# 48 of 256 prompt tokens leave the down product of the PEER layers and join the decoded tokens, by way of DRAM scratch and gathered v rows

## The chip, the core and the metric

The kernel runs on one core of a Trainium2 chip. The metric is the device time of one launch in microseconds (us). The core's engines run side by side: TensorE (PE: matmuls, and PEld, its loads of stationary operands), VectorE (DVE), ScalarE (ACT), GpSimd (POOL) and SyncE (SP, which issues most DMAs). They meet only at semaphores.

## The reference, cut to what matters

Two decoder layers run over 256 prompt tokens and 8 decoded ones (T = 264, D = 1024). Each layer ends in a PEER expert mixer, and its two large products are what the change is about:

```python
def one_block(xb):
    q = einsum('td,de->te', xb, w_q).reshape(128, 8, 2, 128)
    s = einsum('thpc,hpkc->thpk', q, subkeys)
    v1, i1 = top_k(s[:, :, 0], 16); v2, i2 = top_k(s[:, :, 1], 16)
    ...
    eidx = ...                      # 8 heads x 16 = 128 experts of 16384 for each token
    gates = softmax(top_s, axis=-1).reshape(128, 128)
    h = gelu(einsum('td,ted->te', xb, u_tab[eidx]))
    w = gates * h
    return einsum('te,ted->td', w, v_tab[eidx])
```

The result goes through `x <- LayerNorm(alpha*x + f(x))`. `u_tab` and `v_tab` hold 16384 rows of 1024 fp32 numbers for each layer.

## The kernel before, in words

For prompt tokens the kernel does not gather experts. It computes the activation of all 16384 experts for all tokens and multiplies by a gate matrix that is zero but for the chosen ones. The experts are taken as 128 slabs ("rows" below) of 128 experts: a slab is 128x1024 fp32, 512 KB, and a ring of 4 slots holds four. All products are made of three matmuls on split operands (high x high, high x low, low x high; type fp32r), which keeps fp32 accuracy.

`peer_up` makes, slab by slab, `big[:, n, :]` (experts x tokens): ACT writes the high part of the u slab (L2024), POOL the low part (L1930), PE runs 24 matmuls with 264 moving columns (L1972 to L1974) into one of two banks, ACT applies gelu on the way to `big` (L2028, or L2040 and L2041 once gates are there). From slab 52 to 122 the gates of the 256 prompt tokens are formed in 64 groups of four tokens: one-hot matrices on DVE and ACT, a gate product on PE (L1993: 4 fp32 matmuls, which the trace records as 8), ACT and DVE apply it. SP loads the u slabs in order, each as its slot comes free, and at the end of the block the first four v slabs (`load_until`, L203).

`peer_down` multiplies the gated activations of the 256 prompt tokens by the v slabs. Stationary are 128 tokens of `wh`/`wl` (the two parts of `big[:, n, 0:256]`), moving are 512 columns of the v slab's parts `hi`/`lo`: 2 halves x 2 token tiles x 3 = 12 matmuls for a slab (L2386 to L2388). ACT makes `hi` (L2326) and `wh` (L2325), DVE `lo` (L2354) and `wl` (L2350). `hi` has four half-slab buffers, so ACT and DVE run up to two slabs ahead of PE.

The 8 decoded tokens are dealt with apart. Their 128 chosen experts each are spread over 128 partitions as 8 units. ACT copies their activations out of `big` (L2328), SP stores them to a DRAM scratch `decoded_hidden` (L2287), POOL gathers by indirect DMA the v rows (L2304: one unit is 128 rows of 4 KB, 4 buffers) and the activations (L2310: 128 numbers for a unit). DVE, in its program after slab 10, waits for all gathered activations, multiplies them by their gates and builds `own`, 32 stationary columns for each unit. PE adds one unit after each of slabs 12 to 19 (`values`, L2396; unit j writes partitions 32(j%4) and on of banks 6 and 7), and after slab 23 sums the four parts (`add_groups`, L2403). `peer_norm` then copies the prompt result out of banks 0 to 3, transposes it back on PE (L2444), adds the residual (L2449) and normalises.

Each block ends in a barrier of all five engines. Every engine runs its own instructions strictly in the order written; only the semaphores name who waits.

Of the kernel before, what the change touches and what calls it, by code (L numbers as in the profile page):

```python
# [23 lines left out]
F32 = mybir.dt.float32  # L24
F32R = mybir.dt.float32r
# [62 lines left out]
class Step:  # L88


    def __init__(self, nc, io, top):
# [35 lines left out]
        self.hidden = nc.dram_tensor("decoded_hidden", (P, NKEYS * TS), F32, kind="Internal").ap()  # L127
# [1691 lines left out]


def peer(step, layer):
    nc, io, ps = step.nc, step.io, step.ps
    L = f"_{layer}"
    with ExitStack() as ctx:
        big = step.sb("expert_activations" + L, [P, NKEYS, T], ctx=ctx)
        rows = step.sb("decoded_expert_rows" + L, [P, 2, TOPK // 2], U32, ctx=ctx)
        gates = step.sb("decoded_gates" + L, [P, TOPK // 2], ctx=ctx)

        flat = big[:].rearrange("p n t -> p (n t)")
        end = NKEYS * T  # L1830
# [10 lines left out]
GROUPS = TP // GROUP  # L1841
# [14 lines left out]
def peer_up(step, layer, big, qT, scratch, keys_ready, row_index, row_gate):  # L1856
# [9 lines left out]
    gelu_part = step.squares[:, 3:5, 0:TP]  # L1866
# [10 lines left out]
    with ExitStack() as c1, nc.Block("peer_up" + L, no_gpsimd_drain=True) as block:  # L1877
# [4 lines left out]
        row_f = step.sb("decoded_rows_float" + L, [P, 2, TOPK], ctx=c1)  # L1882
        token_of = step.sb("decoded_token" + L, [P, TS], ctx=c1)[:]
# [22 lines left out]
        s_wm = step.sem("activations_gated" + L)  # L1906
        half_done = lambda n, g: 2 * (ub + n) + g + 1

        @block.sync
        def _(sp):  # L1910
            with sp.Fori(1, NKEYS // SLOTS) as i:
                for s in range(SLOTS):

                    sp.wait_ge(step.u_product, half_done(SLOTS * i + s - SLOTS, 1))
                    sp.dma_start(step.ring[:, s, :], io["u"][layer * P + SLOTS * i + s]).then_inc(step.slab_ready[s], 16)
            step.loaded = base + NKEYS
            step.load_until(sp, base + NKEYS + SLOTS)
# [99 lines left out]
        def _(act):  # L2017
# [8 lines left out]
            def gelu(i, s):  # L2026
                act.wait_ge(step.u_product, half_done(SLOTS * i + s, 1))
                nc.scalar.activation(big[:, SLOTS * i + s, :], ps[:, s % 2, 0:T], ACT.Gelu_apprx_tanh).then_inc(s_g, 1)  # L2028

            def gelu_in_parts(n):  # L2030

                gated = GROUP * groups_before(n)
                if gated == 0:
                    gelu(n // SLOTS, n % SLOTS)
# [6 lines left out]
                nc.scalar.activation(big[:, n, gated:T], bank[:, gated:T], ACT.Gelu_apprx_tanh).then_inc(s_g, 1)  # L2041
# [24 lines left out]
            with act.Fori(0, PLAIN // SLOTS) as i:  # L2066
                for s in range(SLOTS):
                    ahead = (i, s + 2) if s < 2 else (i + 1, s - 2)
                    high(*ahead, 0)
                    gelu(i, s)  # L2070
                    high(*ahead, 1)
            act.wait_ge(s_rt, 3)
# [18 lines left out]
        def _(dve):  # L2091
# [79 lines left out]
            for t, (w, heads) in enumerate(((pick[:, 0, 2, :], PH), (pick[:, 1, 2, :], PH), (pick_s[:, 2, :], 1))):  # L2171
# [10 lines left out]
            link(nc.vector.scalar_tensor_tensor(out=row_f[:, 0, :], in0=pick_s[:, 1, :], scalar=float(NKEYS), in1=pick_s[:, 0, :],  # L2182
                                                op0=ALU.mult, op1=ALU.add))
# [387 lines left out]
```

## Time and profile before

| | |
|---|---|
| median of 3 runs | 2500.17 us (2498.72 to 2501.71) |
| profiled execution, its own time | 2500.44 us |
| span of that execution in the trace | 2498.7 us |
| busy of the span | PE 95%, PEld 85%, DVE 67%, ACT 52%, POOL 40% |
| granted TensorE clock, mean | 0.968 of 2.4 GHz |
| bytes moved by DMA | 409.30 MB, 164 GB/s over the span |
| `peer_up` of the two layers, first to last matmul | 441 to 890 us, 1638 to 2088 us |
| `peer_down` of the two layers, first to last matmul | 894.5 to 1275 us, 2092 to 2473 us |

The 1.7 us between the span and the profiled execution's own time lie outside the instructions. Matmuls are pipelined: a record's duration (284 ns for 264 columns) is longer than the distance between two starts, and the distance is what a matmul costs in a row of them.

### The profile page before, as it was taken

What the parts mean: (1) busy time and instruction counts of PE and PEld (TensorE: products, weight loads), DVE (VectorE), ACT (ScalarE), POOL (GpSimd) and SP (SyncE); (2) the same over time, 40 slices, a digit from 0 to 9 for tenths busy, and PEclk for the clock granted to TensorE, in tenths of its full rate; (3) what the DMA queues carried; (4) which work ended last, traced back from release to release, by engine and by line L of the source; (5) the groups of instructions that cost most, each with busy time, mean ns of one, the idle gap of its engine ahead of it and who ended that gap; (6) DMA issues with size and microseconds to landing.
All of it is one profiled execution on the core that took longest, in us unless ns stands there. A gap on an engine that the chain in (4) does not pass through costs nothing. (4 is left out here: it accounts for less than half of the span.)

```text
span 2498.7 us, 46290 instructions
## 1 busy us (share of the span) xinstructions
PE 2361.9 (95%) x15692; PEld 2114.0 (85%) x15692; DVE 1675.8 (67%) x3447; ACT 1290.7 (52%) x2924; POOL 1010.0 (40%) x777
## 2 busy tenths in 40 slices
PE   8798989999999999999979988999999999999997
PEld 8686869999999976888858886999999998688885
DVE  4544748996988844666653454899698894466665
ACT  5221536445776654555543343644577765455554
POOL 4441433898777730000011033479877775000000
PEclk9995999999999999999989989999999999999999
DMA  6333745444444464555535375544444446455552
GB/s 227 131 110 43 261 183 176 148 160 160 141 141 142 142 214 167 186 187 188 185 102 169 100 261 201 180 146 160 162 142 137 143 144 205 167 187 187 187 185 93
DMA packets 115075, 409.30 MB, mean 164 GB/s; under 512 B 19977, under 2 KB 22193, under 8 KB 109489
## 3 DMA queue, kind: packets, MB, share of 16 engines
q1 hardware_dynamic: 110896, 391.45, 47.0%
q0 software_dynamic: 4032, 15.86, 1.9%
q8 instruction: 96, 1.57, 0.3%
q14 instruction: 51, 0.42, 0.1%
HBM read 397.11 MB, written 10.14 MB: 163 GB/s over the span
## 5 line engine op out<-in xcount | busy, mean ns | idle before, releaser
L1930 POOL TENSOR_TENSOR slab_ring_lo<-slab_ring,u_hi 128x512 fp32r<-128x512 f32 x512 | 708.3, 1402 | 203.7 <-ACT u_hi L2024 203.1
L1972 PE MATMUL banks<-operand_hi,u_hi 128*128 128x264 f32 x2048 | 594.6, 290 | 18.5 <-POOL slab_ring_lo L1930 18.4
L1974 PE MATMUL banks<-operand_hi,slab_ring_lo 128*128 128x264 f32 x2048 | 583.1, 285 | 0.0
L1973 PE MATMUL banks<-operand_lo,u_hi 128*128 128x264 f32 x2048 | 581.9, 284 | 0.0
L2354 DVE TENSOR_TENSOR operand_lo<-slab_ring,operand_hi 128x512 fp32r<-128x512 f32 x512 | 354.3, 692 | 134.2 <-ACT operand_hi L2326 129.0
L2386 PE MATMUL banks<-operand_hi,w_hi 128*128 128x512 f32 x1024 | 410.2, 401 | 8.0 <-DVE w_lo L2350 8.0
L309 POOL TENSOR_TENSOR slab_ring_lo<-slab_ring,slab_hi 128x512 fp32r<-128x512 f32 x112 | 146.4, 1308 | 668.8 <-ACT slab_hi L299 668.7
L2388 PE MATMUL banks<-operand_lo,w_hi 128*128 128x512 f32 x1024 | 407.9, 398 | 0.0
L2387 PE MATMUL banks<-operand_hi,w_lo 128*128 128x512 f32 x1024 | 407.8, 398 | 0.0
L1972 PEld LDWEIGHTS banks<-operand_hi,u_hi 128*128 128x128 f32 x2048 | 386.6, 189 | 23.1 <-POOL slab_ring_lo L1930 18.7
L2024 ACT ACTIVATE u_hi<-slab_ring 128x512 fp32r<-128x512 f32 x512 | 321.7, 630 | 159.1 <-PE banks L1974 156.5
L2326 ACT ACTIVATE operand_hi<-slab_ring 128x512 fp32r<-128x512 f32 x512 | 319.3, 624 | 140.6 <-PE banks L2388 140.6
L1973 PEld LDWEIGHTS banks<-operand_lo,u_hi 128*128 128x128 f32 x2048 | 385.5, 188 | 0.0
L1974 PEld LDWEIGHTS banks<-operand_hi,slab_ring_lo 128*128 128x128 f32 x2048 | 385.1, 188 | 0.0
L2386 PEld LDWEIGHTS banks<-operand_hi,w_hi 128*128 128x128 f32 x1024 | 194.1, 190 | 68.4 <-DVE w_lo L2350 21.8
L2388 PEld LDWEIGHTS banks<-operand_lo,w_hi 128*128 128x128 f32 x1024 | 194.1, 190 | 47.5
L2387 PEld LDWEIGHTS banks<-operand_hi,w_lo 128*128 128x128 f32 x1024 | 194.3, 190 | 46.6
L2350 DVE TENSOR_TENSOR w_lo<-expert_activations,w_hi 128x256 fp32r<-128x256 f32 x256 | 108.9, 425 | 164.0 <-ACT w_hi L2325 163.8
L2325 ACT ACTIVATE w_hi<-expert_activations 128x256 fp32r (+1 forms) x256 | 106.8, 417 | 211.5 <-PE banks L2388 211.5
L331 PE MATMUL banks<-operand_hi,slab_hi 128*128 128x264 f32 x496 | 148.3, 299 | 40.9 <-DVE operand_lo L579 15.9
L299 ACT ACTIVATE slab_hi<-slab_ring 128x512 fp32r<-128x512 f32 x220 | 131.4, 623 | 92.5 <-PE banks L333 57.4
L2211 DVE TENSOR_SCALAR one_hot_rows<-constants,squares 128x128 f32<-128x128 f32 x344 | 177.9, 577 | 0.0
(351 smaller groups left out, 4010.7 us busy)
## 6 DMA issues: line engine op xcount, KB each, us to landing
slab_ring<-in_u SPq DMA_DIRECT2D x256, 512.0 KB, 3.3
slab_ring<-in_v SPq DMA_DIRECT2D x256, 512.0 KB, 3.2
slab_ring<-in_proj SPq DMA_DIRECT2D x144, 512.0 KB, 3.3
cache_k_T<-in_cache_k SPq DMA_DIRECT2D x16, 1024.0 KB, 8.8
cache_v<-in_cache_v SPq DMA_DIRECT2D x16, 1024.0 KB, 13.1
memory_T<-in_mem POOLq DMA_DIRECT2D x2, 1024.0 KB, 6.7
sample_state<-in_state POOLq DMA_DIRECT2D x1, 2048.0 KB, 9.1
out_mem_k_out<-mem_k_T SPq DMA_DIRECT2D x16, 128.0 KB, 2.2
```

The lines of the kernel that those rows point to most:

```text
L331: nc.tensor.matmul(out, wh[:, c, :], xh[:, c, :], start=(c == 0), stop=False)
L1930: nc.gpsimd.tensor_tensor(step.ring_lo[:, s, g * HC:(g + 1) * HC, :], step.slab(s)[:, g * HC:(g + 1) * HC, :], hi[:, buf].bitcast(F32), AL ...
L1972: nc.tensor.matmul(bank, hi[:, buf, k, :], xh[:, c, :], start=(c == 0), stop=False)
L1973: nc.tensor.matmul(bank, hi[:, buf, k, :], xl[:, c, :], start=False, stop=False)
L1974: last = nc.tensor.matmul(bank, step.ring_lo[:, s, c, :], xh[:, c, :], start=False, stop=(c == DC - 1))
L2024: nc.scalar.activation(hi[:, buf], step.slab(s)[:, g * HC:(g + 1) * HC, :], ACT.Copy).then_inc(s_hi, 1)
L2211: last = nc.vector.tensor_scalar(rows[g % NB][:, k, :], step.iota, selT[:, 0, token], selT[:, 2, token], ALU.is_equal, ALU.mult)
L2326: nc.scalar.activation(hi[:, (2 * s + g) % 4, :], step.ring[:, s, g * HALF:(g + 1) * HALF], ACT.Copy).then_inc(s_hi, 1)
L2354: nc.vector.tensor_tensor(lo[:, buf, :], step.ring[:, s, g * HALF:(g + 1) * HALF], hi[:, buf, :].bitcast(F32), ALU.subtract).then_inc(step ...
L2386: nc.tensor.matmul(bank, wh[:, b, ts], hi[:, buf, :], start=first, stop=False)
L2387: nc.tensor.matmul(bank, wl[:, b, ts], hi[:, buf, :], start=False, stop=False)
L2388: last = nc.tensor.matmul(bank, wh[:, b, ts], lo[:, buf, :], start=False, stop=final)
```

## The change

`GATHERED = 48` prompt tokens (208 to 255) are treated like the decoded ones in the down product, so that 56 tokens (`GT`) take the gathered way and 208 (`TD`) the dense one.

- `peer_up` still multiplies all 264 columns. Gelu is written in two instructions: columns up to 208 to `big`, the last 56 to a small buffer `part`, which SP stores to the DRAM scratch four slabs at a time (32 stores of 128 x 896 bytes in a layer). SP waits for all stores before it issues the first v slabs.
- Gates are formed for 208 tokens only: 52 groups in place of 64, over the same slabs.
- `peer_down` swaps the operands: stationary are 128 columns of the v slab, moving are 208 tokens, 8 x 3 = 24 matmuls for a slab. The result comes out in the layout of the residual, so the copies and transposes of `peer_norm` are gone.
- There are 56 units in place of 8, gathered into 8 buffers, and added in batches of four, one matmul to each quarter of the partitions: 14 batches, after slabs 26, 33, ..., 117. DVE waits for the 56 gathered activations after its part of slab 23.
- The program of PE for `peer_down` is written out for all 128 slabs, where it had a loop from slab 28.

```diff
-GROUPS = TP // GROUP
+GROUPS = TD // GROUP
...
         @block.sync        # peer_up
...
+            def store(c, half):
+                sp.wait_ge(s_g, SLOTS * c + SLOTS)
+                sp.dma_start(chunk_of[c], part[:, half]).then_inc(s_out, 16)
...
+            for c in range(NKEYS // SLOTS - 2, NKEYS // SLOTS):
+                store(c, c % 2)
+            sp.wait_ge(s_out, 16 * (NKEYS // SLOTS))
             step.loaded = base + NKEYS
             step.load_until(sp, base + NKEYS + SLOTS)
...
+            def gelu_later(n, i, s, half, reused):
+
+                if s == 0 and reused:
+                    act.wait_ge(s_out, 16 * (i - 1))
+                nc.scalar.activation(part[:, half, s, :], ps[:, s % 2, TD:T], ACT.Gelu_apprx_tanh).then_inc(s_g, 1)
...
-OWN_AT, VALUES_FROM, SUM_FROM, UNROLLED = 10, 12, 22, 28
+UNITS = TS + GATHERED
+BATCH = 4
+OWN_AT, BATCH_FROM, BATCH_EVERY = 24, 26, 7
+COPY_AT, ADD_AT, LAST_AT = 120, 122, 124
...
         @block.gpsimd      # peer_down
...
+            for u in range(NB):
+                fetch(u)
+            for u in range(UNITS):
+                nc.gpsimd.indirect_dma_start(hidden[:, u:u + 1], None, hidden_of,
+                                             bass.IndirectOffsetOnAxis(row_index[:, 1, u:u + 1], 0)).then_inc(s_hid, 16)
+            for u in range(NB, UNITS):
+                pool.wait_ge(s_val, (u - NB) // BATCH + 1)
+                fetch(u)
...
         @block.vector      # peer_down
...
+            for n in range(OWN_AT):
+                low(n // SLOTS, n % SLOTS)
...
+            dve.wait_ge(s_hid, 16 * UNITS)
...
+            with dve.Fori(OWN_AT // SLOTS, NKEYS // SLOTS) as i:
                 for s in range(SLOTS):
                     low(i, s)
...
-                    for t in range(2):
-                        bank, ts = ps[:, 2 * t + g, :], slice(t * P, (t + 1) * P)
-                        nc.tensor.matmul(bank, wh[:, b, ts], hi[:, buf, :], start=first, stop=False)
-                        nc.tensor.matmul(bank, wl[:, b, ts], hi[:, buf, :], start=False, stop=False)
-                        last = nc.tensor.matmul(bank, wh[:, b, ts], lo[:, buf, :], start=False, stop=final)
+                    for k in range(HC):
+                        cs = slice(k * P, (k + 1) * P)
+                        out = dense(g * HC + k)
+                        nc.tensor.matmul(out, hi[:, buf, cs], wh[:, b, :], start=(n == 0 and k % 2 == 0), stop=False)
+                        nc.tensor.matmul(out, hi[:, buf, cs], wl[:, b, :], start=False, stop=False)
+                        last = nc.tensor.matmul(out, lo[:, buf, cs], wh[:, b, :], start=False, stop=(n == NKEYS - 1 and k % 2 == 1))
```

How the order of instructions moves is seen at three places. First SP at the end of `peer_up`, where the loads of the first v slabs stand; `in_u` and `in_v` are the expert tables. Before:

```order
L1915 DMA slab_ring<-in_u 128x1024
L1911 REGISTER_ALU
L1911 COMPARE_AND_BRANCH
L203 DMA slab_ring<-in_v 128x1024 x4
L1877 UNCONDITIONAL_BRANCH
L2284 UNCONDITIONAL_BRANCH
L2287 DMA decoded_hidden<-squares 128x1024
```

And SP at the same place with the change:

```order
L1922 DMA slab_ring<-in_u 128x1024 x4
L1926 DMA gathered_hidden<-gathered_hidden_part 128x224 x2
L203 DMA slab_ring<-in_v 128x1024 x4
L1881 UNCONDITIONAL_BRANCH
L2332 UNCONDITIONAL_BRANCH
```

The last stores of activations moved from behind the v loads to ahead of them, and the last of them needs the gelu of slab 127.

Second POOL in `peer_down`: the indirect DMAs that fetch v rows (`in_v`) and activations (into `squares`), first before and then with the change (a row stands for as many instructions as its last number says).

```order
L2296 UNCONDITIONAL_BRANCH
L2298 MEMSET squares 128x256
L2304 DMA gathered_rows<-in_v,decoded_expert_rows 128x1024 x4
L2310 DMA squares<-decoded_hidden,decoded_expert_rows 128x1 x8
L2304 DMA gathered_rows<-in_v,decoded_expert_rows 128x1024 x4
```

```order
L2342 UNCONDITIONAL_BRANCH
L2344 MEMSET own_columns 128x1792
L2349 DMA gathered_rows<-in_v,gathered_expert_rows 128x1024 x8
L2354 DMA squares<-gathered_hidden,gathered_expert_rows 128x1 x56
L2349 DMA gathered_rows<-in_v,gathered_expert_rows 128x1024 x48
```

Ahead of the last activation now stand 8 fetches and 55 gathers where there were 4 and 7, and the memset is seven times as wide.

Third DVE at the end of its part of slab 23, with the change; L2412 is the instruction that waits for all gathered activations (before, its like stood after slab 10).

```order
L2395 TENSOR_TENSOR w_lo<-expert_activations,w_hi 128x208
L2399 TENSOR_TENSOR operand_lo<-slab_ring,operand_hi 128x512
L2412 TENSOR_TENSOR squares<-squares,gathered_gates 128x56
L2415 TENSOR_TENSOR own_columns<-squares 128x8x8
L2417 COPY own_columns<-squares 128x12x4
L2418 UNCONDITIONAL_BRANCH
L2418 ISA
L2399 TENSOR_TENSOR operand_lo<-slab_ring,operand_hi 128x512
```

Behind it in DVE's order stand the low parts of slab 24 and all later ones.

## Rows read from the trace of the kernel before

**Rows 1.** Busy time by stretch: us, busy by engine, clock, DMA share, GB/s

```profile
core 0: us, PE busy (x) PEld busy (x) DVE busy (x) ACT busy (x) POOL busy (x), PEclk, DMA share, GB/s
700.00:800.00 100.00, 100.00 (x840) 100.00 (x839) 86.46 (x161) 69.74 (x193) 72.44 (x54) 1.00 0.44 143
...
892.00:930.00 38.00, 35.49 (x141) 28.45 (x142) 23.84 (x43) 21.21 (x41) 12.35 (x13) 0.91 0.73 246
```

**Rows 2.** Timeline of the down product: start, us, engine, line, operation

```profile
1099.92 0.39 PE L2386 MATMUL banks<-operand_hi,w_hi 128*128 128x512 f32 x1
...
1110.47 0.39 PE L2386 MATMUL banks<-operand_hi,w_hi 128*128 128x512 f32 x1
```

**Rows 3.** Timeline of the up product, a slab with a gate product

```profile
801.35 0.28 PE L1973 MATMUL banks<-operand_lo,u_hi 128*128 128x264 f32 x1
...
804.05 0.28 PE L1974 MATMUL banks<-operand_hi,slab_ring_lo 128*128 128x264 f32 x1
804.05 0.98 PEld L1993 LDWEIGHTS banks<-one_hot_columns,one_hot_rows 128*128 128x128 f32 x8
...
804.95 0.19 PEld L1972 LDWEIGHTS banks<-operand_hi,u_hi 128*128 128x128 f32 x1
...
805.06 0.19 PEld L1973 LDWEIGHTS banks<-operand_lo,u_hi 128*128 128x128 f32 x1
...
805.18 0.28 PE L1973 MATMUL banks<-operand_lo,u_hi 128*128 128x264 f32 x1
```

**Rows 4.** Weight loads of 32 columns in attention: ns min/median/max

```profile
L1684 PEld LDWEIGHTS banks<-cache_k_T,sample_own_rows x256: 106/110/110, 317.3 to 1528.4; 128*32 128x32 f32 x128
```

**Rows 5.** Timeline of PE in attention, matmuls to four partition quarters in turn

```profile
317.35 1.93 PE L1684 MATMUL banks<-cache_k_T,sample_own_rows 128*32 128x256 f32 x32
```

**Rows 6.** Timeline of PE around a unit of the decoded tokens

```profile
933.38 0.40 PE L2388 MATMUL banks<-operand_lo,w_hi 128*128 128x512 f32 x1
933.71 1.90 PE L2396 MATMUL banks<-gathered_rows,squares 128*32 128x512 f32 x4
935.54 0.50 PE L2386 MATMUL banks<-operand_hi,w_hi 128*128 128x512 f32 x1
```

**Rows 7.** Timeline from the last gelu to the first down matmul

```profile
890.83 0.17 ACT L2041 ACTIVATE expert_activations<-banks 128x8 f32<-128x8 f32 x1
...
892.78 0.61 ACT L2326 ACTIVATE operand_hi<-slab_ring 128x512 fp32r<-128x512 f32 x1
...
894.51 0.80 PE L2386 MATMUL banks<-operand_hi,w_hi 128*128 128x512 f32 x1 [4.00 <-DVE w_lo L2350]
```

**Rows 8.** DMA issues: engine, count, KB each, median us to landing

```profile
slab_ring<-in_v SPq DMA_DIRECT2D x256, 512.0 KB, 3.2
...
out_mem_k_out<-mem_k_T SPq DMA_DIRECT2D x16, 128.0 KB, 2.2
...
squares<-decoded_hidden,decoded_expert_rows POOLq DMA_INDIRECT x16, 4.2
```

**Rows 9.** Timeline of POOL in the down block, both layers

```profile
891.81 0.31 POOL L2298 MEMSET squares<- 128x256 f32 x1 [4.75 <-POOLq L1877]
892.59 1.05 POOL L2304 DMA_INDIRECT gathered_rows<-in_v,decoded_expert_rows  x1 [0.47 <-POOL squares L2298]
...
898.01 0.95 POOL L2310 DMA_INDIRECT squares<-decoded_hidden,decoded_expert_rows  x1 [0.30 <-issue]
...
906.91 1.26 POOL L2310 DMA_INDIRECT squares<-decoded_hidden,decoded_expert_rows  x1 [0.30 <-issue]
...
2096.16 0.99 POOL L2310 DMA_INDIRECT squares<-decoded_hidden,decoded_expert_rows  x1 [1.02 <-DMA decoded_hidden<-squares]
...
2106.21 0.94 POOL L2310 DMA_INDIRECT squares<-decoded_hidden,decoded_expert_rows  x1 [0.30 <-issue]
```

**Rows 10.** Timeline of the tail, layer 1, up to the mean's subtraction

```profile
2473.27 1.29 DVE L2431 COPY expert_activations<-banks 128x512 f32<-128x512 f32 x2 [4.28 <-PEq L2260]
...
2474.47 0.21 DVE L2432 SCALAR_TENSOR_TENSOR res_peer<-x_T,squares 128x64 f32<-128x64 f32 x1
...
2481.38 2.80 DVE L395 TENSOR_TENSOR res_peer<-res_peer,banks 128x264 f32<-128x264 f32 x8 [0.81 <-PE banks L380]
```

More of the change, by code:

```diff
@@ L1865, in peer_up @@
     selT = step.squares[:, 0:3, 0:TP]
-    gelu_part = step.squares[:, 3:5, 0:TP]
+    gelu_part = step.squares[:, 3:5, 0:TD]
     at = 2 * PH * P
@@ L1910, in _, with load @@
         def _(sp):
[L1911 to L1915, printed above, removed]
+            chunk_of = step.hidden.rearrange("p (c s) t -> c p s t", s=SLOTS)
+            def load(i, s):
+                sp.wait_ge(step.u_product, half_done(SLOTS * i + s - SLOTS, 1))
+                sp.dma_start(step.ring[:, s, :], io["u"][layer * P + SLOTS * i + s]).then_inc(step.slab_ready[s], 16)
+            def store(c, half):
+                sp.wait_ge(s_g, SLOTS * c + SLOTS)
+                sp.dma_start(chunk_of[c], part[:, half]).then_inc(s_out, 16)
+            with sp.Fori(0, NKEYS // SLOTS // 2 - 1) as ii:
+                for half in range(2):
+                    for s in range(SLOTS):
+                        load(2 * ii + 1 + half, s)
+                    store(2 * ii + half, half)
+            for s in range(SLOTS):
+                load(NKEYS // SLOTS - 1, s)
+            for c in range(NKEYS // SLOTS - 2, NKEYS // SLOTS):
+                store(c, c % 2)
+            sp.wait_ge(s_out, 16 * (NKEYS // SLOTS))
             step.loaded = base + NKEYS
@@ L2065, in _, with plain @@
                     high(0, s, g, first=True)
-            with act.Fori(0, PLAIN // SLOTS) as i:
+            def plain(i, half, reused):
                 for s in range(SLOTS):
@@ L2069, in _ @@
                     high(*ahead, 0)
-                    gelu(i, s)
+                    gelu(i, s, half, reused)
                     high(*ahead, 1)
+            for i in range(2):
+                plain(i, i, False)
+            with act.Fori(1, PLAIN // SLOTS // 2) as ii:
+                for half in range(2):
+                    plain(2 * ii + half, half, True)
             act.wait_ge(s_rt, 3)
@@ L2452, in peer_down, with gathered_residual @@
-        emit_norm(step, block, "peer" + L, layer * 3 + 2, res, (0, 1), residual_steps, transposes,
-                  step.used if layer + 1 < LAYERS else None, {"scalar": scalar_early, "vector": vector_early})
+        def gathered_residual(dve):
+            nc.vector.scalar_tensor_tensor(out=res[:, :, TD:T], in0=step.x[:, :, TD:T], scalar=ALPHA, in1=y_g,
+                                           op0=ALU.mult, op1=ALU.add)
+        def residual_steps(dve, j):
+            return nc.vector.scalar_tensor_tensor(out=res[:, j, 0:TD], in0=step.x[:, j, 0:TD], scalar=ALPHA,
+                                                  in1=dense(j), op0=ALU.mult, op1=ALU.add)
```

222 lines of the change are left out of this document (101 added, 121 removed).

## The prediction

> **What bounds the kernel now.** I read the busy times by stretch first. PE is busy for all of 100 us in the middle of the up product and for 35.49 of 38 us at the start of the down product, at a granted clock of 1.00 (2.4 GHz) and 0.91 [rows 1]. So TensorE sets the pace, and the question is what a slab costs on it. That comes from the timeline, by distances between starts. In the down product 45 matmuls of 512 columns pass between 1099.92 and 1110.47, 0.2344 us each [rows 2], 12 of them 2.813 us a slab. In the up product 22 distances of 264 columns take 2.70 us, 0.1227 us each, and a slab with a gate product takes 805.18 - 801.35 = 3.83 us against 24 x 0.1227 = 2.945 without, so a group costs PE 0.885 us [rows 3]. Both widths stream 2.15 to 2.18 columns a ns. The other engines matter where PE waits for them: at the seam between the two products [rows 7] and at whatever the gathered way makes late.
>
> **The change part by part, for one layer.** The sum is made against the profiled execution's 2500.44 us (span 2498.7 and 1.7 outside), which is 0.3 above the median, so I count the two as equal.
>
> 1. *The dense product.* 24 x 208 = 4992 columns take the place of 12 x 512 = 6144. By columns alone a matmul would cost 208 / 2.185 = 0.095 us. But there are now 24 loads of 128 stationary columns, not 12. The eight loads of a gate group start at 804.05 and the next load at 804.95, 0.1125 us apart, though their matmuls have only 128 columns; two fp32r loads behind them start 0.11 apart (804.95, 805.06) [rows 3]. A load seems to go on at that rate beside matmuls, and at 264 columns it is just hidden (0.1227). At 208 columns it no longer is. I take 0.111 us, between the two: 2.664 us a slab, 0.149 less than now. With the two slabs that run at the half clock left out (parts 5 and 6), 126 x 0.149 = **-18.8 us**. Bounds: 0.095 below (columns alone), 0.1227 above (208 columns should not cost more than 264).
>
> The load itself can be priced in another way: a load of 128 columns shows 0.19 us [rows 3], one of 32 columns 0.110 [rows 4], so 96 columns cost 0.080 and 128 cost 0.107 us, if nothing is lost between loads. A slab would be 2.56 us, 13.1 us less in a layer than by 0.111. The Trainium skill, "TensorE: Matmul & The Clock Gate", section "LDWEIGHTS (loading the stationary operand)", puts a load at its column count over 1.2 GHz, whatever the contraction; for 128 columns that is 0.1067 us, and an estimate of the slab by it would be 2.56 us. The row of back-to-back loads says 0.1125, so I stay at 0.111 and make the lower figure a rival.
>
> 2. *Units on PE.* One unit costs 935.54 - 933.38 - 0.234 = 1.93 us now [rows 6], 8 make 15.4. A batch issues 8 matmuls, two for each partition quarter. In attention, 32 records of 256 columns that go to the four quarters in turn take 1.93 us together [rows 5]; one after the other at the same rate they would take several times that, so four run at once. A batch should then cost what a unit costs, 1.95 us. 14 batches are 27.3: **+11.9 us**. Were they serial, a batch would be four units, 7.7 us: +92.
>
> 3. *Gates.* 12 groups fewer on a PE that is full there [rows 1]: 12 x 0.885 = **-10.6 us**.
>
> 4. *Up product otherwise.* ACT gets a second gelu instruction, at least 0.17 us (8 columns) [rows 7]. ACT is busy for 69.74 of 100 us there and PE does not wait [rows 1], so the cover is PE's own 2.9 us a slab; uncovered it would be 128 x 0.17 = 22 us. What is delayed by 0.17 us is the second high part of a u slab and so POOL. I take **+0.5**.
>
> 5. *The seam.* Now the v slabs are in flight when the last gelu ends at 891.00, the first high part starts at 892.78 and PE at 894.51, 1.73 later [rows 7]. After the change SP cannot issue them until the last store has landed. A store of 128 KB lands in 2.2 us, a slab in 3.2 [rows 8]: 891.0 + 2.2 + 3.2 + 1.73 = 898.1, plus 0.1 for issue: **+3.7 us**. The clock loss of the first slabs (0.91 over 38 us, 3.4 us at most, some of it idle [rows 1]) stays; I call it 2.5.
>
> 6. *The gathered activations.* This is the step that a look at bytes misses. POOL restarts 0.8 us after the last engine is done (891.81 against 891.00 [rows 7, 9]), now behind SP: about 894.0. Memset of seven times the columns: 7 x 0.31 = 2.2, and 0.47 to the first DMA: 896.7. Eight fetches at (898.01 - 892.59) / 4 = 1.355 us: 907.5. Activations come at (906.91 - 898.01) / 7 = 1.271 us apart in layer 0 and (2106.21 - 2096.16) / 7 = 1.436 in layer 1, mean 1.354 [rows 9]. 56 of them: 75.8 us, to 983.3, the last landing 4.2 after its start [rows 8]: 986.2. DVE then makes `own` (0.6 us) and the first low part of slab 24 (1.1): PE can start slab 24 at 987.9. It would have arrived at 898.2 + 2.5 + 24 x 2.664 = 964.6. So PE stands still for 23.3 us, and restarts at the half clock, 2.5 more: **+25.8 us**. Behind DVE's wait stand all later low parts, behind them PE, v_split, and with it SP's next v slabs. Bounds: at 1.271 us the stall is 18.7 + 2.5, at 1.436 27.9 + 2.5. Nothing hides it: ACT and DVE are at most two slabs ahead.
>
> 7. *DMA.* In the batch phase 7 slabs and 4 units, 11 x 0.524 MB, pass in 7 x 2.664 + 1.95 = 20.6 us: 280 GB/s. At the start of the down product 246 GB/s kept the DMA engines 0.73 busy [rows 1], which gives about 337 at full share. I take 0, and keep the possibility.
>
> 8. *Tail.* Now 2481.38 - 2473.27 = 8.11 us from the first copy to the mean's subtraction [rows 10]. Without copies and transposes DVE has one instruction of 448 columns (0.21 for 64 [rows 10], so about 0.6) and 8 additions, with the mean's matmuls behind them: about 4.6. **-3.5 us**.
>
> Sum: -18.8 + 11.9 - 10.6 + 0.5 + 3.7 + 25.8 - 3.5 = +9.0 us a layer, +18.0 for two: **2518 us**, 0.7% slower.
>
> **The rivals.**
> - *A load costs 0.107 us.* For it: the differences of durations [rows 3, 4]. Against: the eight loads at 0.1125. 13.1 us less on slabs, but PE arrives 2.5 us earlier at the same wait: -10.6 a layer, 2497 us. By the page's 0.1067 it is the same time to a microsecond. Chance 0.12.
> - *Columns set the pace (0.095 us).* For it: 512 and 264 columns cost the same per column. Against: loads have never been seen closer than 0.11. Slab 2.28 us: 48.4 less, 9.2 given back in the wait, -39 a layer: 2440 us, less whatever DMA (5.77 MB in 17.9 us, 322 GB/s) takes back. This is the side other than mine: faster. It decides from 0.107 us a matmul downward. Chance 0.10.
> - *The wait for activations is not there,* because POOL keeps a much closer pace in a long row of equal gathers. At the measured pace no slack is near; it needs 0.94 us, POOL's busy part alone, or less. Then 56 take 53 us, and the stall ends: 2518 - 52 = 2466 us. Chance 0.06.
> - *DMA becomes the bound.* If 246 GB/s is all that is to be had, 7 slabs take 23.5 us, 2.9 more, 13 times: +37 a layer, 2593 us; with half of that 2555. For it: 280 GB/s is over anything in these rows. Against: the 0.73. Chance 0.11.
> - *Loads and moving columns disturb each other,* or the longer written-out program of PE and ACT's added work cost something, up to the 0.1227 of the up product: 126 x 0.28 = +35 on slabs, -7 in the wait: 2575 at the bound, 2545 midway. Chance 0.08.
>
> **How the numbers follow.** My own case has 0.53 and spans 2502 to 2532 (load 0.109 to 0.1125, gather pace 1.27 to 1.44). 0.2%, 5 us, is about what a measurement of this kernel can tell from no change. Faster by more than that are the column rival, the missing wait and half of the load rival: 0.22. Within it: the other half and the lowest edge of mine: 0.08. Slower: 0.70. The range 2493 to 2545 leaves out 0.16 below and the worse part of DMA and disturbance above; this is a little more than 0.2, and I do not widen it for tails whose sizes are bounds.
>
> **What the changed profile would show.** Starts of the down matmuls 0.11 us apart (part 1); batches of about 1.95 us (2); up slabs with a gate product still at 3.83 but 52 of them (3); first down matmul about 7.5 us after the last gelu (5); POOL's gathers in one row for 75 us and PE idle for 18 to 28 us before slab 24 in each layer, with the wait put down to DVE and DVE's to the gathered activations (6); a DMA share above 0.8 in the batch phase with no wait of ACT for v slabs (7). The prediction falls if the matmul distance is outside 0.109 to 0.113, or if PE shows no stop at slab 24.

## The result and the profile after

The changed kernel takes 2515.36 us (median of 5 runs, 2510.72 to 2518.71), the kernel before 2498.89 us beside it (median of 5, 2498.40 to 2501.71). The ratio is 1.0061 with a 95% interval of 1.0047 to 1.0076: slower by 0.6%. The forecast was 2518 us, with 0.70 on slower.

The first view is the page of the changed kernel: busy time by engine, and three lines of its 40 slices (TensorE's granted clock, the DMA engines' busy share, GB/s).

```profile
span 2515.3 us, 52721 instructions
...
PE 2333.5 (93%) x18924; PEld 2212.8 (88%) x18924; DVE 1572.0 (62%) x3328; ACT 1259.2 (50%) x3078; POOL 1207.8 (48%) x969
...
PEclk9895989999999998999989989999999999899999
DMA  6333745555455474888735374545545546488872
GB/s 221 127 117 42 261 177 180 153 165 170 160 151 160 142 263 150 279 279 278 244 109 167 104 262 191 182 151 168 176 151 152 159 154 243 142 279 281 277 254 100
```

The down products are the slices with 278 to 281 GB/s and a DMA share of 0.8. By stages, read off the two traces as the starts of the first and last dense matmuls, in us:

| stage | before | after | change | forecast |
|---|---|---|---|---|
| up to the first up matmul | 441.25 | 443.68 | +2.4 | 0 |
| up product, layers 0 and 1 | 448.98, 449.33 | 438.16, 438.13 | -10.8, -11.2 | -10.1 |
| last up matmul to first down matmul | 4.28, 4.28 | 7.62, 7.75 | +3.3, +3.5 | +3.7 |
| down product | 380.19, 380.48 | 398.46, 397.47 | +18.3, +17.0 | +18.9 |
| tail, then the stages up to the next up product or the end | 363.63, 26.25 | 361.21, 22.84 | -2.4, -3.4 | -3.5 |

They sum to 16.6 us, the difference of the spans. In the 12 runs below, nothing ahead of the first up matmul differs from the changed kernel, yet that stretch took from 439.4 to 446.2 us. So the +2.4 of the first row is inside what two executions differ by.

The windows of the changed kernel, which answer to [rows 1]; the third is in the middle of the down product, the fourth is the restart at slab 24:

```profile
core 0: us, PE busy (x) PEld busy (x) DVE busy (x) ACT busy (x) POOL busy (x), PEclk, DMA share, GB/s
700.00:800.00 100.00, 100.00 (x839) 100.00 (x839) 70.99 (x140) 68.47 (x212) 73.90 (x58) 1.00 0.52 156
892.00:930.00 38.00, 38.00 (x336) 38.00 (x336) 24.20 (x44) 21.32 (x42) 29.46 (x29) 0.98 0.85 303
1010.00:1110.00 100.00, 100.00 (x888) 93.83 (x889) 58.78 (x101) 51.69 (x102) 21.02 (x20) 1.00 0.82 281
976.00:981.00 5.00, 4.92 (x23) 4.92 (x24) 2.81 (x6) 0.63 (x1) 0.00 (x0) 0.50 0.58 152
```

PE is full wherever it is not stopped. 303 GB/s passed in the second window and PE did not wait, and in the batch phase 281 GB/s passed at a full clock, so the DMA rival has nothing to stand on.

The timeline of PE in the changed kernel: the restart at slab 24, a batch of units (against [rows 6]), and two starts with 95 other dense matmuls between them (against [rows 2]).

```profile
976.08 0.54 PE L2433 MATMUL banks<-w_hi,operand_hi 128*128 128x208 f32 x1 [20.20 <-DVE w_lo L2395]
...
986.97 0.27 PE L2435 MATMUL banks<-w_hi,operand_lo 128*128 128x208 f32 x1
987.17 1.92 PE L2446 MATMUL banks<-gathered_rows,own_columns 128*32 128x512 f32 x16
989.03 0.36 PE L2433 MATMUL banks<-w_hi,operand_hi 128*128 128x208 f32 x1
...
1012.59 0.28 PE L2433 MATMUL banks<-w_hi,operand_hi 128*128 128x208 f32 x1
...
1023.31 0.28 PE L2433 MATMUL banks<-w_hi,operand_hi 128*128 128x208 f32 x1
```


From 1012.59 to 1023.31 are 10.72 us, over 96 distances 0.1117 us a matmul, 2.681 us a slab. The batch takes 989.03 - 986.97 - 0.11 = 1.95 us here; over all of them the slab that ends in a batch takes 4.62 us and the next 2.77, so a batch costs 4.62 + 2.77 - 2 x 2.68 = 2.03 us.

The waits of the changed kernel (engine, what waited, on what; total us, times, longest us):

```profile
DVE squares L2412 <- DMA squares<-gathered_hidden,gathered_expert_rows: 42.0, 2, 22.3
```

This is the wait of step 6. DVE stands 22.3 us in layer 0 and the rest of 42.0 in layer 1, and PE 20.2 us behind it. The seam and POOL's row of gathers, in the timelines of ACT, SP and POOL (against [rows 7] and [rows 9]):

```profile
882.40 0.21 ACT L2051 ACTIVATE gathered_hidden_part<-banks 128x56 f32<-128x56 f32 x1
887.77 0.63 ACT L2370 ACTIVATE operand_hi<-slab_ring 128x512 fp32r<-128x512 f32 x1 [5.16 <-DMA slab_ring<-in_v]
```

```profile
882.64 0.35 SPq L1926 DMA_DIRECT2D gathered_hidden<-gathered_hidden_part  x1
884.36 1.76 SPq L203 DMA_DIRECT2D slab_ring<-in_v  x4
```

```profile
886.90 1.59 POOL L2344 MEMSET own_columns<- 128x1792 f32 x1 [8.23 <-POOLq L1881]
888.65 1.39 POOL L2349 DMA_INDIRECT gathered_rows<-in_v,gathered_expert_rows  x1 [0.16 <-issue]
...
899.70 0.95 POOL L2354 DMA_INDIRECT squares<-gathered_hidden,gathered_expert_rows  x1 [0.30 <-issue]
...
972.12 0.94 POOL L2354 DMA_INDIRECT squares<-gathered_hidden,gathered_expert_rows  x1 [0.30 <-issue]
```

The 56 gathers of activations start from 899.70 to 972.12, (972.12 - 899.70) / 55 = 1.317 us apart, and DVE goes on at 974.57.

### The profile page after: what moved, and what is told of

The parts are those of the page before. It is cut to its first block and busy times, and to the rows that moved or that the text cites. A ratio compares the mean times of both kernels' runs of the same rounds, so it can differ in the third digit from the quotient of the medians.

```text
span 2515.3 us, 52721 instructions
## 1 busy us (share of the span) xinstructions
PE 2333.5 (93%) x18924; PEld 2212.8 (88%) x18924; DVE 1572.0 (62%) x3328; ACT 1259.2 (50%) x3078; POOL 1207.8 (48%) x969
## 5 line engine op out<-in xcount | busy, mean ns | idle before, releaser
L2433 PE MATMUL banks<-w_hi,operand_hi 128*128 128x208 f32 x2048 | 569.6, 278 | 52.6 <-DVE w_lo L2395 52.6
L1993 PE MATMUL banks<-operand_hi,u_hi 128*128 128x264 f32 x2048 | 592.1, 289 | 18.9 <-POOL slab_ring_lo L1951 18.6
L2434 PE MATMUL banks<-w_lo,operand_hi 128*128 128x208 f32 x2048 | 569.2, 278 | 0.0
L2435 PE MATMUL banks<-w_hi,operand_lo 128*128 128x208 f32 x2048 | 565.5, 276 | 0.0
L2433 PEld LDWEIGHTS banks<-w_hi,operand_hi 128*128 128x128 f32 x2048 | 398.3, 194 | 76.8 <-DVE w_lo L2395 76.8
L2434 PEld LDWEIGHTS banks<-w_lo,operand_hi 128*128 128x128 f32 x2048 | 398.3, 194 | 0.0
L2435 PEld LDWEIGHTS banks<-w_hi,operand_lo 128*128 128x128 f32 x2048 | 398.2, 194 | 0.0
L2349 POOL DMA_INDIRECT gathered_rows<-in_v,gathered_expert_rows x112 | 117.8, 1051 | 404.3 <-PE banks L2446 377.7
L2369 ACT ACTIVATE w_hi<-expert_activations 128x208 fp32r (+1 forms) x256 | 96.5, 377 | 198.4 <-PE banks L2435 198.4
L331 PE MATMUL banks<-operand_hi,slab_hi 128*128 128x264 f32 x496 | 148.5, 299 | 42.5 <-DVE operand_lo L579 16.2
L2395 DVE TENSOR_TENSOR w_lo<-expert_activations,w_hi 128x208 fp32r<-128x208 f32 x256 | 96.1, 375 | 139.7 <-ACT w_hi L2369 139.5
```

Source lines behind the costliest of these rows:

```text
L331: nc.tensor.matmul(out, wh[:, c, :], xh[:, c, :], start=(c == 0), stop=False)
L1993: nc.tensor.matmul(bank, hi[:, buf, k, :], xh[:, c, :], start=(c == 0), stop=False)
L2433: nc.tensor.matmul(out, hi[:, buf, cs], wh[:, b, :], start=(n == 0 and k % 2 == 0), stop=False)
L2434: nc.tensor.matmul(out, hi[:, buf, cs], wl[:, b, :], start=False, stop=False)
L2435: last = nc.tensor.matmul(out, lo[:, buf, cs], wh[:, b, :], start=False, stop=(n == NKEYS - 1 and k % 2 == 1))
```

## The experiments

All stand against the changed kernel. "Distance" is from the start of one dense down matmul to the next.

### The activations are wanted later

```diff
-OWN_AT, BATCH_FROM, BATCH_EVERY = 24, 26, 7
+OWN_AT, BATCH_FROM, BATCH_EVERY = 36, 38, 6
```

> DVE's wait for the gathered activations stands after slab 35, the 14 batches after slabs 38, 44, ..., 116; nothing else is changed. My theory: the stop before slab 24 (20.4 and 17.7 us, and 2.9 and 3.3 us more in the two slabs behind it at the half clock) goes and nothing takes its place, because POOL's gathers are over by then: 44 us less, 2471 us, and the down product about 375 us a layer. Rival: the v rows and slabs, now closer together, are bound by DMA (91 slabs' worth in less time); then PE waits for v slabs in the batch phase and part of the gain is given back, 2485 to 2510 us. Rival 2: the wait only moves to slab 36, and the time stays at 2515.

Measured: 2470.21 us (2466.16 to 2473.43, 4 runs) beside 2500.52 for the kernel before, ratio 0.9881 (0.9865 to 0.9898). The waits have no row of DVE on a DMA of `squares` any more, the down products take 375.1 and 374.9 us instead of 398.5 and 397.5. So the wait of step 6 cost 23.0 us a layer, restart included (25.8 in the forecast), and all of it was a matter of when the activations are asked for. With it gone the change is 1.2% faster than before.

### The activations are gathered first

```diff
-            for u in range(NB):
-                fetch(u)
             for u in range(UNITS):
                 nc.gpsimd.indirect_dma_start(hidden[:, u:u + 1], ...)
+            for u in range(NB):
+                fetch(u)
```

> POOL issues the 56 gathers of activations ahead of the 8 first fetches of v rows. My theory: the stop is set by POOL's own row of DMAs, so it shortens by the 8 fetches, about 11 us in each layer: 2493 us, PE idle before slab 24 for 9 and 7 us. Rival: the stop is set by the landing of the gathers behind traffic (slabs and rows share the DMA engines); then it shortens by more or less than 11 us, or not at all.

Measured: 2496.63 us (one run). The row of waits, which was 42.0 in total, is now:

```profile
DVE squares L2412 <- DMA squares<-gathered_hidden,gathered_expert_rows: 24.3, 2, 12.2
```

Eight fetches ahead of the gathers were worth (42.0 - 24.3) / 2 = 8.9 us a layer in the wait and 9.8 in the down product, where 11 had been expected. In the changed kernel the fetches take 899.70 - 888.65 = 11.05 us, but here the gathers start 1.335 and 1.340 us apart instead of 1.317 and 1.310, which over 55 takes back 1.3 us. The remaining 12 us are the row of 56 gathers itself. So the arithmetic of POOL's queue holds; the pace of its row is not quite a constant.

### The v loads are issued before the stores have landed

```diff
-            for c in range(NKEYS // SLOTS - 2, NKEYS // SLOTS):
-                store(c, c % 2)
-            sp.wait_ge(s_out, 16 * (NKEYS // SLOTS))
             step.loaded = base + NKEYS
+            store(NKEYS // SLOTS - 2, 0)
             step.load_until(sp, base + NKEYS + SLOTS)
+            store(NKEYS // SLOTS - 1, 1)
+            sp.wait_ge(s_out, 16 * (NKEYS // SLOTS))
```

> SP issues the first four v slabs ahead of the last store and of the wait for all stores. My theory: of the seam's 7.6 us the part behind the v slabs' landing goes; what is left is the last store's landing (about 1.8 us), the barrier and 1.7 us to the first matmul: about 5 us, so 2.6 us less in each layer, 2510 us. But PE then arrives at slab 24 earlier, and POOL starts no earlier, so if DVE's wait sets the time of slab 24, the gain is lost in the wait and the time stays at 2515. I expect the second: the same time, a seam of 5 us and a stop that is 2.5 us longer.

Measured: 2515.77 us (2514.69 to 2516.32, 4 runs), ratio 1.0060 (1.0043 to 1.0077): nothing gained, as expected. DVE's wait at `squares` rose from 42.0 to 44.3 us. But the seam fell only from 7.6 and 7.8 to 6.9 and 6.7 us, where 2.6 less had been expected, so the next run asks what else is in it.

### Both edits

The two diffs above together.

> Both edits together: the gathered activations are wanted at slab 36 instead of 24, and the first v loads stand ahead of the last store and of the wait for the stores. Theory (v loads ahead of the stores were worth nothing in the run before only because the down product then waited that much longer for the gathered activations): with no such wait left, the 2.7 us that the seam loses show in the end, 2 layers: 2470.2 - 5.4 = 2465. Rival (the seam is not on the path, or starting the v stream earlier only moves a wait to a later slab): 2470, as with the later units alone.

Measured: 2469.43 us (2467.86 to 2471.26, 4 runs), ratio 0.9866 (0.9850 to 0.9882). Against the later units alone, whose interval overlaps, nothing can be told; the seams are 0.8 and 1.3 us shorter in the trace. The theory of the seam is wrong in part. In the timeline the last gelu starts at 884.15 (0.21 long), the v slabs are issued from 880.99 on, and ACT still starts its first high part only here:

```profile
888.75 0.63 ACT L2370 ACTIVATE operand_hi<-slab_ring 128x512 fp32r<-128x512 f32 x1 [4.39 <-PEq L1881]
```

L1881 is the up product's block. All engines leave it together, and SP leaves it last, for it waits for the store. Three views: how long a store takes to land, in the rows of the scratch tensor of the changed kernel; SP's waits in this one; and its stores' landing.

```profile
DMA to landing us min/median/max: 1.7/3.5/4.6
```

```profile
SPq L1881 <- DMA gathered_hidden<-gathered_hidden_part: 6.4, 2, 3.2
```

```profile
DMA to landing us min/median/max: 3.3/3.5/4.9
```

In the changed kernel SP issued the v slabs 1.7 us after its last store, and 1.7 is the shortest landing of one; with v slabs ahead of it none landed in under 3.3. So the store took back 1.6 us of the 2.6 or 2.7 that the early v loads were expected to give.

### The store is waited for by POOL

The version with 16 gathered tokens (below), and in it SP's wait for the stores goes to the engine that reads them.

```diff
@@ SP, end of the up product
-            sp.wait_ge(s_out, 16 * (NKEYS // SLOTS))
@@ POOL, down product, between the fetches and the gathers
+            pool.wait_ge(s_out, 16 * (NKEYS // SLOTS))
```

> The version with 16 gathered prompt tokens, and in it SP no longer waits for its stores at the end of the up product: POOL waits for them in the down product, ahead of its gathers of activations. Theory (with the v loads early, the seam is still 6.5 us, because the up product's block ends only when the last store has landed; the first high part starts 4.4 us after the last gelu and 1.8 in the kernel before): the seam falls to about 4.3 us, 2.3 less in each layer, 2455.1 - 4.6 = 2450.5, and POOL's wait costs nothing because the store has landed long before the fetches are issued. Rival (something else in the block's end takes the time, such as the v slabs' own landing or SP's issue times): 2455.

Measured: the seam is 3.35 us instead of 6.65, more than expected, and the kernel still got slower, 2506.51 us (2499.55 to 2510.96, 10 runs) against 2455.12 without this edit. Both down products are 26.4 us longer. In slab 3 PE changes from a distance of 0.11 us to one of 0.7 and more, with no semaphore behind it ("issue"). Timeline of PE:

```profile
908.02 0.28 PE L2435 MATMUL banks<-w_hi,operand_lo 128*128 128x240 f32 x1
908.21 0.27 PE L2433 MATMUL banks<-w_hi,operand_hi 128*128 128x240 f32 x1
908.94 0.27 PE L2434 MATMUL banks<-w_lo,operand_hi 128*128 128x240 f32 x1 [0.46 <-issue]
909.64 0.37 PE L2435 MATMUL banks<-w_hi,operand_lo 128*128 128x240 f32 x1 [0.44 <-issue]
910.34 0.27 PE L2433 MATMUL banks<-w_hi,operand_hi 128*128 128x240 f32 x1 [0.32 <-issue]
```

I call this the crawl. It was run again, unchanged:

> The same kernel as e10_poolwait_g16, run again on whatever chip is given. In its trace, and in those of e7_serial and e11_narrow176 from the same chip, TensorE crawled in slabs 3 and 4 of both down products, one load and matmul each 2.1 to 2.8 us, for as long as POOL's row of activation gathers lasted; up to slab 24 the last two run the changed kernel's own program, which did not crawl on its chip. Theory (the crawl belongs to that chip and its state, not to the kernel's edits): here slabs 3 and 4 take 2.7 us and the time is the 2450.5 expected before (seam 3.4 instead of 6.5 us, 2455.1 - 2 x 3.1 = 2449). Rival (the crawl comes with this kernel, because POOL's wait or the earlier start puts the gathers on top of something): 2506 again.

Measured: 2505.04 us (2500.32 to 2506.28, 12 runs), on another chip than the run before. The crawl is there again: slab 3 takes 28.2 us in layer 0 and 22.7 in layer 1. The theory written down there, that it belongs to one chip, has fallen. (Of the two other kernels named there only the one whose batches go quarter by quarter has the changed kernel's program up to slab 24; the other has 176 moving columns.) More of it in the last section.

### More tokens in the dense product, fewer in units

```diff
-GATHERED = 48
+GATHERED = 16        # in the others 32, 4
-OWN_AT, BATCH_FROM, BATCH_EVERY = 24, 26, 7
+OWN_AT, BATCH_FROM, BATCH_EVERY = 24, 26, 15        # 28, 30, 9 and 24, 26, 30
```

With 16 and 4 the unit buffers `NB` are 4 instead of 8; all three have the early v loads.

> 16 prompt tokens are gathered and 48 join the dense part's prompt side, so that the dense matmuls have 240 moving columns instead of 208 and there are 6 batches of units instead of 14, and 60 groups of gates instead of 52; the unit buffers are 4 instead of 8. Theory (the dense matmul is bound by the load of its 128 stationary columns, 0.1117 us, and 240 columns take 0.111 or less at the 2.15 to 2.19 columns per ns that the 256 and 512 column matmuls show): the distance stays 0.1117 and a layer changes by 8 batches fewer x 2.03 = -16.2 and 8 groups more x 0.885 = +7.1, -9.1; from 2465 to 2447. Rival (columns and load both count: each column costs 0.111/208 = 0.00053 us): the distance grows to 0.128, 128 slabs x 24 x 0.0166 = +51 a layer, 2549. Units begin at slab 26, the gathers are a third as many on POOL, so no wait is expected at slab 24.

> 32 prompt tokens gathered, 224 moving columns, 10 batches and 56 groups. By the theory of the load (0.1117 us whatever the columns up to about 240): a layer changes by -4 x 2.03 + 4 x 0.885 = -4.6 against 48 gathered, two layers -9.2, 2456. By the rival of a price per column: +0.0083 x 24 x 128 = +25 a layer, 2506.

> 4 prompt tokens gathered, 252 moving columns, 3 batches and 63 groups. By rate the matmul of 252 columns takes 0.115 to 0.117 us, 3.3 to 5.3 ns over the load's 0.1117: 128 x 24 x 0.0043 = +13.2 a layer; 11 batches fewer = -22.3, 11 groups more = +9.7: about +0.6 a layer against 48 gathered, 2466, and 10 to 19 more than with 16 gathered. If the load alone set the distance up to 256 columns, it would be 2465 - 25 = 2440.

Measured: 16 gathered 2455.12 us (2454.39 to 2456.94), ratio 0.9810 (0.9794 to 0.9826); 32 gathered 2458.15 (2457.91 to 2460.64), ratio 0.9823 (0.9806 to 0.9839); 4 gathered 2478.47 (2477.67 to 2480.31), ratio 0.9906 (0.9889 to 0.9922); 4 runs each. Two starts that are 96 distances apart, in PE's timeline for 32, 16 and 4 gathered in turn:

```profile
992.47 0.28 PE L2433 MATMUL banks<-w_hi,operand_hi 128*128 128x224 f32 x1
...
1003.19 0.28 PE L2433 MATMUL banks<-w_hi,operand_hi 128*128 128x224 f32 x1
```

```profile
997.13 0.27 PE L2433 MATMUL banks<-w_hi,operand_hi 128*128 128x240 f32 x1
...
1007.94 0.27 PE L2433 MATMUL banks<-w_hi,operand_hi 128*128 128x240 f32 x1
```

```profile
1000.28 0.28 PE L2433 MATMUL banks<-w_hi,operand_hi 128*128 128x252 f32 x1
...
1011.61 0.28 PE L2433 MATMUL banks<-w_hi,operand_hi 128*128 128x252 f32 x1
```

That is 0.1117 us at 224 columns, 0.1126 at 240 and 0.1180 at 252. With 0.1117 at 208 and 0.1227 at 264 [rows 3], the price is flat up to 224 and then follows the columns: 240, 252 and 264 of them pass at 2.13 to 2.15 a ns. The rival of a price per column (2506 us for 32 gathered, 2549 for 16) is refuted. The 8 us that 16 gathered fell short of 2447 are the 0.0009 us a matmul (2.8 us a layer) and an up product 8.3 us longer, not 7.1. The 12 that 4 gathered fell short of 2466 are 0.0063 us a matmul over the load instead of 0.0043 (6.2 a layer).

### 128 moving columns

```diff
-nc.tensor.matmul(out, hi[:, buf, cs], wh[:, b, :], ...)
+nc.tensor.matmul(out[:, 0:128], hi[:, buf, cs], wh[:, b, 0:128], ...)        # and so the other two
```

> The dense down product has only 128 moving columns in its 24 matmuls (tokens 128 to 207 are left out of it); ACT, DVE and all loads are as before. My theory: loads of 128 stationary columns set the distance of the matmuls, so it stays at 0.1117 us, a slab at 2.68, and the time at 2515. Rival, columns set the distance at 0.457 ns each: 0.058 us, a slab at 1.4 us or whatever ACT and DVE then allow (about 1.8), and over 150 us less in the slabs, part of it eaten by a longer stop before slab 24.

Measured: 2604.64 us (one run), 89 slower than the changed kernel instead of equal to it. The timeline shows why that does not speak for columns:

```profile
1054.17 0.27 PE L2433 MATMUL banks<-w_hi,operand_hi 128*128 128x128 f32 x1
...
1064.89 0.27 PE L2433 MATMUL banks<-w_hi,operand_hi 128*128 128x128 f32 x1
```

96 distances are 10.72 us again, 0.1117 each: with 80 columns fewer the distance is the same to the last digit. So the moving columns do not set it. No run varied the stationary columns; that the fixed price is their load rests on the eight loads 0.1125 us apart in [rows 3]. The time was lost to the clock, by the windows:

```profile
900.00:950.00 50.00, 50.00 (x236) 50.00 (x236) 17.31 (x32) 14.46 (x29) 38.16 (x39) 0.50 0.43 137
960.00:1000.00 40.00, 40.00 (x190) 40.00 (x189) 14.09 (x24) 12.21 (x24) 6.86 (x7) 0.50 0.33 99
1100.00:1150.00 50.00, 50.00 (x446) 46.99 (x446) 30.22 (x52) 26.45 (x52) 8.34 (x8) 1.00 0.83 281
```

From the first slab to the first batch of units PE is busy for all of the time and has a granted clock of 0.50 (1.2 GHz); a slab takes 5.12 us, 0.2133 a matmul. 26 such slabs cost 63 us a layer more, and the 20.4 us of PE's stop at slab 24 are gone, since PE comes later than the activations: +43 a layer, as measured (441.0 against 398.5). Behind the first batch the clock is 1.00 again and stays there, with seven slabs of the same narrow matmuls between two batches.

### 176 moving columns

The same edit with 176 for 128.

> As the kernel with 128 moving columns in the dense down product, but with 176 (tokens 176 to 207 are left out of the product), to see from what width the granted clock falls there. By the load, the matmul distance at the full clock stays 0.112 us. If the clock follows how wide the matmuls are, it is between the 0.957 of 208 columns and the 0.914 of 128 over the run, and the time between 2515 and 2604; if the width alone is not the cause, the time is 2515.

Measured: 2727.00 us (one run). Slabs 5 to 25 take 5.1 us here too, at a granted clock of 0.50, and 2.7 once units have begun; the changed kernel's was 0.98 from 892 to 930. So at 176 columns the clock behaves as at 128, not halfway between 128 and 208. The 123 us over the expected bound of 2604 are the crawl: slabs 3 and 4 take 47.8 and 26.7 us in layer 0, 18.3 and 56.0 in layer 1.

### A batch quarter by quarter

```diff
-                for g in range(2):
-                    for q in range(BATCH):
+                for q in range(BATCH):
+                    for g in range(2):
```

> The eight matmuls of a batch of units are issued quarter by quarter (two on one quarter, then two on the next) instead of one half for all four quarters and then the other. Theory (matmuls on different partition quarters run at once, those on the same quarter one after another): a batch has four pairs that follow each other on a quarter, of which only the neighbours overlap: it costs more than the 2.03 us of the changed kernel, by the 0.234 us of a 512-column matmul three times over about 0.7 us, 14 batches in 2 layers +20, less what the wait at slab 24 does not see (all batches are behind it): 2535. Rival (order on the queue does not matter, or the quarters never ran at once): 2515 as the changed kernel.

Measured: 2619.97 us (one run), again with the crawl, so the time says nothing of the edit. The batch does, in PE's timeline:

```profile
1035.57 0.28 PE L2435 MATMUL banks<-w_hi,operand_lo 128*128 128x208 f32 x1
1035.78 1.94 PE L2446 MATMUL banks<-gathered_rows,own_columns 128*32 128x512 f32 x16
1037.65 0.36 PE L2433 MATMUL banks<-w_hi,operand_hi 128*128 128x208 f32 x1
```

1.97 us from 1035.57 + 0.11, against 1.95 in the old order. By whole slabs a batch costs 4.65 + 2.77 - 2 x 2.68 = 2.06 us, against 2.03. The expectation was wrong: the order does not matter. In the trace the 16 records of a batch start in four clusters of four, 0.43 us apart, and inside a cluster 0.013 us apart (0.007 in the old order). So four matmuls run side by side in either order, and each is done in two passes. The loads that wait for the v rows of the second, third and fourth quarter start 0.013 us apart behind the first quarter's load, and the matmuls of the first cluster start 0.002 us behind these four loads. In the program the first quarter's second matmul stands before them. So across partition quarters PE does not keep the order written, as was said of every engine at the start, and this is why the order here makes no difference.

## Why the prediction was right

It was right in sign, size and, for the most part, by its steps.

1. *The dense product*, -18.8 a layer. The distance was 0.1117 us, not 0.111; 126 x (2.813 - 2.681) = -16.6. The choice of the row with back-to-back loads over the difference of two durations was right, and the widths 128, 208 and 224 show a price that the moving columns do not touch, 0.1117 us at each. The Trainium skill, "TensorE: Matmul & The Clock Gate", section "LDWEIGHTS (loading the stationary operand)", gives 0.1067 us by its rule; in nine kernels with 128 to 224 columns the median distance was 0.111 or 0.112, so the measurement decides. At the half clock the distance was 0.2133 us, twice that figure; at the full clock it is 5 ns over it. The rival with 0.107 and the one with 0.095 are out.
2. *Units*, 27.3 us for 14 batches: 14 x 2.03 = 28.4. That four run at once, which rested on attention's rows alone, was right. A unit in the kernel before cost 2.03 us too by whole slabs (the prediction read 1.93 off one gap, and the slab behind a unit is 0.1 longer), so 8 were 16.2, not 15.4, and the term is +12.2.
3. and 4. *Gates and the up product*: -10.1 forecast, -10.8 and -11.2 measured. The +0.5 for the second gelu does not show.
5. *The seam*, +3.7: +3.3 and +3.5. The sum was right, the reason only in part. I had the v loads' flight behind the store as the whole of it. In the runs the early v loads gave 0.7 to 1.3 us; what holds the down product is that the up product's block ends only with the store's landing. Taking that out gave 2.9 to 3.3 us more.
6. *The gathered activations*, +25.8: 23.0 by the kernel that wants them at slab 36. PE stood 20.4 and 17.7 us, not 23.3, and lost 2.9 and 3.3 us behind it at the half clock, not 2.5. The terms that were off are small: the gathers were 1.317 us apart in layer 0, not 1.354, 2.0 us over 55, and DVE went on 2.45 us after the start of the last, not 4.2; against this the first gather came 0.9 us later after the first down matmul than forecast.
7. *DMA*, 0: right for the time, at up to 303 GB/s. ACT did wait for a v slab five times outside the start of a block, 0.5 to 2.0 us each, two of them in the batch phase, where the forecast profile had none. None of it reached PE, whose slabs there stayed at 2.68 us.
8. *Tail*, -3.5: -3.4 in layer 1 and, with the stages behind it, -2.4 in layer 0.

By whole slabs the down product adds up. All 127 distances between slabs: -16.8. Units: +12.2. Wait and restart: +23.3 in layer 0, +21.0 in layer 1. The first slabs at the half clock: -0.6 and +0.4. Together +18.1 and +16.8, against 18.3 and 17.0 measured.

That the total came so near is in part luck. The slabs gave 2 us a layer less than forecast, and the wait with its restart cost 2.5 and 4.8 us less; these two nearly cancel. Of the 16.6 us measured, 2.4 lie ahead of the first up matmul, where the program is the same. The stages that the change touches gave +14.2, against +18.0 forecast.

The change as written gives away what its idea holds. Its own gains (slabs, gates, tail) are about 31 us a layer; the units cost 12, the seam 3.4, and the wait 21 to 23. One line of numbers turns +0.6% into -1.2%. With 16 tokens gathered instead of 48, 4 buffers and the early v loads it is -1.9%, the fastest kernel that was run (2455.12 us).

## What to carry to other kernels

- From 128 to 224 moving columns an fp32r matmul with a new 128-column stationary operand cost 0.112 us at the full clock, whatever the columns. So columns taken out below that can be put back: here 16 more tokens in the dense part cost the matmuls nothing and 32 more 2.8 us a layer, and they saved units at 2.03 us a batch. With 128 and 176 columns the half clock, 0.213 us a matmul, cost far more than the load.
- Where many small gathers stand in one row, multiply their number by the distance of their starts (1.25 to 1.35 us here), and compare with the time at which the first consumer arrives. Moving the consumer 12 slabs back was worth 45 us.
- An edit ahead of such a wait shows nothing in the time. The early v loads could be judged by the seam in the trace alone; with the wait gone they were worth 0.8 and 1.3 us there, too little for the timed runs to tell. And a wait at the end of a block holds back all engines, not the one that needs the data.

## What the runs showed of the hardware that was not expected

**A busy PE at the half clock.** With 128 moving columns the granted clock was 0.50 for some 130 us of uninterrupted matmuls, up to the first batches of units, and 1.00 behind them; with 176 it was the same through slabs 5 to 25. In the changed kernel, with 208 in the same place, it was 0.98. Nearly all down products begin at the half clock. With 208 columns and more PE left it within the first two slabs, with 128 and 176 only once matmuls of 512 columns came in between. What about the narrow matmuls holds it there no run shows. At 0.50 the distance is 0.213 us at every width from 128 to 252 columns, so the clock matters to a row that is bound by loads as to any other.

**The crawl.** In four traces, of three kernels, PE in slabs 3 and 4 issued one load and matmul every 0.7 to 2.8 us, mostly in multiples of 0.70 us, while POOL's row of activation gathers lasted. It was back at its pace within 4 to 11 us of the row's end, in both layers. In all eight down products the run of slow steps began between the 82nd and the 90th dense matmul (in one a single slow step came at the 72nd), 1 to 10 us after the row's start; so the row's start alone does not set it off. In the quarter-by-quarter kernel the timeline of PE, then of POOL, then the window, read:

```profile
934.29 0.33 PE L2433 MATMUL banks<-w_hi,operand_hi 128*128 128x208 f32 x1 [2.47 <-issue]
937.09 0.33 PE L2434 MATMUL banks<-w_lo,operand_hi 128*128 128x208 f32 x1 [2.47 <-issue]
939.89 0.33 PE L2435 MATMUL banks<-w_hi,operand_lo 128*128 128x208 f32 x1 [2.47 <-issue]
```

```profile
897.18 0.95 POOL L2354 DMA_INDIRECT squares<-gathered_hidden,gathered_expert_rows  x1 [0.30 <-issue]
...
965.84 0.94 POOL L2354 DMA_INDIRECT squares<-gathered_hidden,gathered_expert_rows  x1 [0.30 <-issue]
```

```profile
906.00:966.00 60.00, 7.89 (x25) 6.68 (x25) 1.76 (x3) 1.53 (x3) 45.37 (x49) 0.50 0.05 9
```

The DMA engines are almost idle (share 0.05), so it is not bandwidth. ACT is slowed too: it waits up to 30.5 us in this stretch for signals that the trace cannot assign. POOL alone is quicker than elsewhere: its gathers are (965.84 - 897.18) / 55 = 1.248 us apart, against 1.317 in the changed kernel. It looks as if POOL's row and the other engines' instructions and signals compete for something and POOL wins, but that is argued, not shown. A rival that no run tested is the fetching of PE's written-out program: from 906 to 966 us the DMA view of the changed kernel lists five instruction packets, that of the quarter-by-quarter kernel none, which may be cause or consequence. What sets the crawl off stays open. It was, by two traces and by the times, in every run of the kernel whose POOL waits for the store (22 timed, two chips) and in the two kernels that were run beside it, of which the one whose batches go quarter by quarter has up to slab 24 nothing that differs from the changed kernel; the eight kernels on the other two chips (six of them timed four times each) never had it, by their traces and times. The kernel before ran at its usual 2502 and 2504 us on the two chips that showed the crawl. Kernel and chip cannot be told apart by these: the edit to POOL's wait alone does not explain the other two, and one bad chip does not explain the repeat on another. It would take the changed kernel and the POOL-wait kernel side by side on one chip that has shown the crawl and on one that has not. By the difference of the down products to those with 16 gathered (28.2 and 27.5 us), the POOL-wait kernel without the crawl would be at 2505.0 - 55.7 = 2449 us; this is an estimate.
